# A mixture-of-experts stage on one core: the expert weights stand in TensorE instead of the rows, and each expert moves as many rows as its place in a ranking allows

## What is computed

```python
N_EXPERTS, TOP_K, EXPERT_FF, MOE_BLOCK = 64, 6, 256, 128
def _routed_experts(xt, eidx, gates, w_gate, w_up, w_down):
    ...
    def step(acc, blk):
        tok, g, e = blk
        xb = xpad[tok]
        hid = jax.nn.silu(xb @ w_gate[e]) * (xb @ w_up[e])
        yb = (hid @ w_down[e]) * g[:, None]
        return acc.at[tok].add(yb.astype(acc.dtype)), None
```

## Time and profile before

| what | us |
|---|---|
| median of three runs | 2301.89 |
| the profiled execution's own time | 2310.06 |
| its span in the profile | 2307.7 |
| PE busy in the span | 2164.2 (94%) |
| DVE, ACT, POOL busy | 1405.2, 1129.7, 645.4 |

### The profile page before, as it was taken

The page is one execution under the profiler, slowest core; times in us unless marked ns, Lnnn a source line. Parts: engine busy times, 40 slices in busy tenths (PEclk is TensorE's granted clock), DMA queues, the critical chain, the costliest instruction groups (busy, mean ns, idle before and its releaser), DMA issues. The chain is left out here.

```text
span 2307.7 us, 34429 instructions
## 1 busy us (share of the span) xinstructions
PE 2164.2 (94%) x10800; PEld 1766.7 (77%) x10800; DVE 1405.2 (61%) x2590; ACT 1129.7 (49%) x1866; POOL 645.4 (28%) x597
## 2 busy tenths in 40 slices
PE   6999999999899999959999999999999999999970
PEld 5777778777678888747888888888888888888850
DVE  5444444444677877746666666666666666666638
ACT  4344334433533333215556565555655565655537
POOL 1111111111113233332333333333333333333310
PEclk9999999999899999969999999999999999999995
DMA  6101101012623323247999989999999998999958
GB/s 218 40 31 34 41 32 37 34 41 84 244 67 107 101 81 109 93 161 224 284 286 279 277 275 285 281 280 281 280 287 284 284 278 276 275 286 280 282 110 323
DMA packets 194561, 435.84 MB, mean 189 GB/s; under 512 B 35488, under 2 KB 40080, under 8 KB 193200
## 3 DMA queue, kind: packets, MB, share of 16 engines
q1 hardware_dynamic: 150928, 289.49, 36.8%
q0 software_dynamic: 43312, 144.90, 23.6%
q10 hardware_dynamic: 288, 1.05, 0.1%
HBM read 328.16 MB, written 109.39 MB: 190 GB/s over the span
## 5 line engine op out<-in xcount | busy, mean ns | idle before, releaser
L1706 PE MATMUL ex_psU<-ex_guh,ex_xh 128*128 128x512 f32 x1024 | 413.8, 404 | 3.7 <-DVE ex_xl L1691 3.7
L1708 PE MATMUL ex_psU<-ex_guh,ex_xl 128*128 128x512 f32 x1024 | 402.6, 393 | 0.0
L1707 PE MATMUL ex_psU<-ex_gul,ex_xh 128*128 128x512 f32 x1024 | 400.5, 391 | 0.0
L1555 POOL DMA_INDIRECT acc_d<-ex_y,ex_use x128 | 206.3, 1612 | 410.1 <-ACT ex_y L1618 348.9
L1708 PEld LDWEIGHTS ex_psU<-ex_guh,ex_xl 128*128 128x128 f32 x1024 | 193.1, 189 | 43.3
L1706 PEld LDWEIGHTS ex_psU<-ex_guh,ex_xh 128*128 128x128 f32 x1024 | 193.3, 189 | 40.7 <-DVE ex_xl L1691 4.3
L1707 PEld LDWEIGHTS ex_psU<-ex_gul,ex_xh 128*128 128x128 f32 x1024 | 193.9, 189 | 37.5
L1577 POOL DMA_INDIRECT ex_xg<-h_d,entries x128 | 199.3, 1557 | 59.2 <-issue 38.1
L1706 PE MATMUL ex_psY<-ex_dnh,ex_hdh 128*128 128x512 f32 x512 | 210.2, 411 | 1.7 <-DVE ex_hdl L1662 1.7
L1618 ACT ACTIVATE ex_y<-ex_psY 128x1024 f32<-128x1024 f32 x128 | 131.3, 1025 | 143.3 <-PE ex_psY L1708 143.3
L1708 PE MATMUL ex_psY<-ex_dnh,ex_hdl 128*128 128x512 f32 x512 | 200.0, 391 | 0.0
(11 more groups left out here) (351 smaller groups left out, 4400.1 us busy)
## 6 DMA issues: line engine op xcount, KB each, us to landing
mi_g_raw<-w_experts SPq DMA_DIRECT2D x96, 1024.0 KB, 11.8
mi_g_place<-w_experts SPq DMA_DIRECT2D x96, 1024.0 KB, 11.8
mi_xr<-xT SPq DMA_DIRECT2D x17, 512.0 KB, 3.5
acc_d<-de_acc SPq DMA_DIRECT2D x17, 512.0 KB, 13.3
h_d<-de_h POOLq DMA_DIRECT2D x17, 512.0 KB
ln_t<-acc_d SPq DMA_DIRECT2D x17, 512.0 KB, 5.8
y<-ln_t SPq DMA_DIRECT2D x17, 512.0 KB, 4.4
de_cr<-cat SPq DMA_DIRECT2D x16, 512.0 KB
```

The lines of the kernel that those rows point to most:

```text
L1555: nc.gpsimd.indirect_dma_start(out=io["acc_d"], out_offset=bass.IndirectOffsetOnAxis(ap=use[:, k, 0:1].bitcast(U32), axis=0), in_=y[:, k, ...
L1706: nc.tensor.matmul(out, lh, rh, start=start, stop=False)
L1707: nc.tensor.matmul(out, lh, rl, start=False, stop=False)
L1708: return nc.tensor.matmul(out, ll, rh, start=False, stop=stop)
```

## The change

**Ranking.** The dense stage's end sorts the experts by their number of rows (two small products and some ten small DVE operations more, before the list of further blocks). Experts 0 and 1 keep the places 0 and 1, since their weights are loaded before the ranks are known; the other 62 follow by rising count. Each place has a capacity; an expert with more rows than its place takes gets further blocks of 256.

```diff
-OVMAX = 50
+OVMAX = 64
 OVP = OVMAX // 2
+MORE = NE + 2 * OVMAX
+CLASSES = ((1, 6, 176), (6, 13, 192), (13, 18, 208), (18, 23, 220), (23, 27, 236), (27, 32, 256))
+CAPS = [BLK] * 2 + [n for begin, end, n in CLASSES for _ in range(2 * (end - begin))]
...
-            sp.wait_ge(S["blocks_dve"], 3)
+            sp.wait_ge(S["blocks_dve"], 5)
```

(begin, end) are pairs of places, the third number is the capacity n of both places of such a pair. `pairs` writes pair 0 out and then, for each class, its first pair, and loops over the others of the class:

```diff
+            pair(0, BLK, BLK, None)
+            before = BLK
+            for begin, end, n in CLASSES:
+                peeled = 1
+                pair(begin, before, n, None)
+                if end > begin + peeled:
+                    with eng.Fori(begin + peeled, end) as p:
+                        pair(p, n, n, None)
+                before = n
```

SP reads the number of the expert from the table of the order (a value load for each expert), and takes weights that lie in DRAM as 8 KB in one piece for each partition instead of four pieces of 2 KB:

```diff
-                        w = io["w_experts"][bass.ds(e, 1), kind].rearrange("o k p n -> (o p) k n")
-                        sp.dma_start(raw[b][:, kind].rearrange("p (k n) -> p k n", k=4), w).then_inc(s_w[b][kind], 16)
+                        w = io["w_experts"][bass.ds(e, 1), kind].rearrange("o p n -> (o p) n")
+                        sp.dma_start(raw[b][:, kind], w).then_inc(s_w[b][kind], 16)
```

POOL keeps its order; the second gather and the second addition of an expert have n - 128 rows instead of 128 (`rows_of`):

```diff
+        rows_of = lambda n, t: P if t == 0 else n - P
...
                         nc.gpsimd.indirect_dma_start(
-                            out=xg[:, k, :], out_offset=None, in_=io["h_d"],
-                            in_offset=bass.IndirectOffsetOnAxis(ap=ent[:, k, 0:1].bitcast(U32), axis=0)).then_inc(s_row[k], 16)
+                            out=xg[0:r, k, :], out_offset=None, in_=io["h_d"],
+                            in_offset=bass.IndirectOffsetOnAxis(ap=ent[0:r, k, 0:1].bitcast(U32), axis=0)).then_inc(s_row[k], 16)
```

PE: in gate and up the weights stand and the rows move, n at once; the hidden values come out already transposed, so hidden_T and psH are gone. The unit of PE's order is now an expert, in two halves f of the hidden width:

```diff
+            def gate_up(e, b, f, n):
+                if not exists(e):
+                    return
+                if f == 0:
+                    pe.wait_ge(s_xl, 2 * e + 2)
+                after(pe, s_hid, 2 * e + f - 1)
+                for half in range(2):
+                    c0 = half * FF + f * P
+                    for kc in range(KC):
+                        if f == 0 and half == 0 and kc % 2 == 0:
+                            pe.wait_ge(s_split, 6 * e + kc // 2 + 1)
+                        last = three(psU[:, f, half, 0:n], guh[:, b, kc, c0:c0 + P], gul[:, b, kc, c0:c0 + P],
+                                     xh[:, kc, 0:n], xl[:, kc, 0:n], kc == 0, kc == KC - 1)
                 last.then_inc(s_gu, 1)
...
+            def pair(p, n1, n, j):
+                for b in range(2):
+                    e = 2 * p + b
+                    gate_up(e - 1, 1 - b, 1, n if b else n1)
+                    transpose_x(p, e, b)
+                    down(e - 2, b, n1)
+                    gate_up(e, b, 0, n)
```

```diff
+            def pair(p, n1, n, j):
+                for b in range(2):
+                    e, m = 2 * p + b, n if b else n1
+                    sigmoid(e - 1, 0, m)
+                    round_w(p, e, b, (0, 1))
+                    hidden(e - 1, 0, 1 - b, m)
+                    round_w(p, e, b, (2, 3))
+                    sigmoid(e - 1, 1, m)
+                    round_x(e, 0, n)
+                    hidden(e - 1, 1, 1 - b, m)
+                    round_x(e, 1, n)
+                    output(e - 2, b, range(4), n1)
+                    round_w(p, e, b, (4, 5))
```

More of the change, by code:

```diff
@@ L1648, in _, with sigmoid @@
-            end = pairs(act, pair)
-            n = 4 * end
-            hidden(n - 2)
-            sigmoid(n - 1, 3)
-            output(n - 2, 2, False)
-            hidden(n - 1)
-            output(n - 1, 3, False)
+            A = nc.scalar.activation
+            def sigmoid(e, f, n):
+                if exists(e):
+                    act.wait_ge(s_gu, 2 * e + f + 1)
+                    after(act, s_hid, 2 * e + f - 1)
+                    A(sg[:, f, 0:n], psU[:, f, 0, 0:n], ACT.Sigmoid).then_inc(s_sig, 1)
@@ L1656, in _ @@
+            e = 2 * pairs(act, pair)
+            sigmoid(e - 1, 0, BLK)
+            hidden(e - 1, 0, 1, BLK)
+            sigmoid(e - 1, 1, BLK)
+            output(e - 2, 0, range(2), BLK)
+            hidden(e - 1, 1, 1, BLK)
+            output(e - 2, 0, range(2, 4), BLK)
+            output(e - 1, 1, range(4), BLK)
         @block.vector
@@ L1701, in _ @@
+            e = 2 * pairs(dve, pair)
+            for f in range(FC):
+                activate(e - 1, f, BLK)
+                hidden(e - 1, f, 1, BLK)
         @block.tensor
@@ L1734, in down @@
+            def down(e, b, n):
+                if not exists(e):
+                    return
+                pe.wait_ge(s_hl, 2 * e + 2)
+                pe.wait_ge(s_split, 6 * e + 6)
+                for u in range(4):
+                    t, half = u // 2, u % 2
+                    r = rows_of(n, t)
+                    after(pe, s_y, 4 * e + u - 1)
                     for f in range(FC):
-                        last = three(psY[:, cols], hdh[:, f, :], hdl[:, f, :], dnh[:, b, f, cols], dnl[:, b, f, cols],
+                        last = three(psY[0:r, half, :], hdh[:, b, f, t * P:t * P + r], hdl[:, b, f, t * P:t * P + r],
+                                     dnh[:, b, f, half * 512:(half + 1) * 512], dnl[:, b, f, half * 512:(half + 1) * 512],
@@ L1760, in _, with pair @@
-            end = pairs(pe, pair)
-            n = 4 * end
-            hidden_T(n - 2, 2)
-            gate_up(n - 1, 3, 1, 12 * end - 2)
-            down(n - 2, 1, 12 * end)
-            hidden_T(n - 1, 3)
-            down(n - 1, 1, 12 * end)
+                    last.then_inc(s_dn, 1)
+            def pair(p, n1, n, j):
+                for b in range(2):
+                    e = 2 * p + b
[3 more added lines that the diff above has]
+                    gate_up(e, b, 0, n)
@@ L1770, in stage_norm @@
+            e = 2 * pairs(pe, pair)
+            gate_up(e - 1, 1, 1, BLK)
+            down(e - 2, 0, BLK)
+            down(e - 1, 1, BLK)
 def stage_norm(nc, io):
```

324 lines of the change are left out of this document (144 added, 180 removed).

## The result

The kernel became **slower**: 2362.05 us at the median (four runs, 2354.63 to 2365.87) beside 2304.33 for the kernel before on the same chips, a ratio of 1.024 with a 95% interval of 1.0221 to 1.0259. Forecast were 2272, in a range of 2225 to 2345. The profiled execution has a span of 2352.9 us.

The account below looks back on a forecast made before the run. PE was taken to bound the expert stage, with the DMA engines close behind. Experts save 36 + 1 us, the stage's ends cost 4 and 3: 30 less than the median of 2301.89 gives 2272 us, range 2225 to 2345.

Parts of the forecast that it names:

- p: Distance on PE between two gate and up products: 0.112 us under 256 columns, 0.119 at 256.
- Rivals 2, 3 and 5: Product distances on PE: 0.097 us, about 2243 (chance 0.13); 0.119 throughout, 2306 (0.09); 0.174, about 2580 (0.06).
- 7.2 + 96 p: PE's time for one expert: down products and transposes 7.2 us, plus 96 gate and up products; 17.95 for narrower experts.
- Gathers landing in under 6 us behind the additions: POOL's row gathers in the expert loop, with weights issued behind them, were expected to land in under 6 us.
- rival 1: Gathers, issued on POOL after additions, come too late if landing takes over 6.0 us; about 2530 at 10.4; chance 0.20.
- rival 4: Second gathers and additions of 92 rows use 4 of 16 DMA engines: 35 to 60 us, about 2315; chance 0.10.
- The sum: Expert stage's total: 37 us gained over the experts, less 4 and 3 at its ends, 30 us less in all.
- The ends: Start and end of the expert stage: 4 us more at the start, 3 us more at the end.
- The ranking and the layout at no cost: Ranking operations hidden before the table's entries load; 8 KB weight pieces costed at nothing, since nothing waits for weights.

Follow-up runs that it names:

- experiment 4: Changed kernel, second gather and addition both rounded up to 96 and 112 rows, capacities 220 and 236 kept: 2281.7 us, ratio 0.9912 to the kernel before.
- experiment 8: Kernel before with only the weights' layout changed, 8 KB in one piece instead of four of 2 KB: 2302.81 us, ratio 0.9992.
- experiment 1: Changed kernel with capacities 220 and 236 raised to 224 and 240: 2287.11 us, ratio 0.9914 to the kernel before.
- experiment 7: Changed kernel with only two classes, 52 experts with 240 rows and the others with 256: 2300.22 us, ratio 0.9992 to the kernel before.

## Why the prediction was wrong, point by point

- **p, right.** Forecast 0.112 under 256 columns and 0.119 at 256; measured 0.111 to 0.112 for 176 to 240, and 0.120. The reading that the load of the stationary operand sets it fits: the width makes no difference below 256 columns. The estimate of 0.107 by the Trainium skill (TensorE: Matmul & The Clock Gate, LDWEIGHTS (loading the stationary operand)) is close below. Rivals 2, 3 and 5 are out.
- **7.2 + 96 p, right, with an error of 0.1.** Forecast 17.95, measured 18.05 in the first three classes. Over the 52 narrow experts experiment 4, where nothing else disturbs, takes 941.9 us against 970.0 before: 28 saved, forecast 36. Some 5 of the 8 missing us lie in those 0.1, the others in the classes of 220 and 236, at 18.2 and 18.4.
- **Gathers landing in under 6 us behind the additions, right for the good row counts only in its effect.** In experiment 4 a gather takes 4.2 to 7.7, 6.1 at the median, so about half take longer than forecast; PE waits 2.2 us in all. The weights are indeed issued behind them. The deciding point of rival 1, a landing of 6 us, is where its waits begin; so it has no slack, and that is why rival 4 hit so hard.
- **The failed step: the row counts.** The sum has no term for them, which puts a transfer of 92 or 108 rows at the price of 128 in proportion; they stand in rival 4 alone, with a chance of 0.10. The mechanism was written down rightly there, 92 rows on 4 engines. The Trainium skill's rule (DMA: Bandwidth & Descriptors, Why a DMA increments its semaphore by 16 and not by 1) holds for these indirect transfers by GpSimd: 4 engines for 92 and 76 rows are slow, 10 for 100 a little, 12 to 15 for 108, 52, 60 and 84 hardly or not. Its exception for some direct copies from GpSimd doesn't reach them. The rival's price was too low, 3.5 to 6 us for each of 10 experts. The two slow transfers follow each other and hold up the gather of 128 rows between them (landings 6 to 10.9), two experts behind the class still pay, and a wait of 4.1 us costs 1.7 us more by the clock. Measured: 66.7 us over twelve experts, beside experiment 4. The forecast of 2272 with that is 2339, with the 8 us above and the 3 below 2350; of the 12 left, 2.7 are in the class of 236 (113.2 us for its last six experts, 110.5 in experiment 4), 2 are that before ran at 2304 on these chips, not 2302, and 7 are that the 66.7 come from an execution of 2354.63 us, 7.4 below the median.
- **The ends, 7 forecast, about 10 measured** in experiment 4: the stage from the load of the entries to the next stage takes 1211.35 us instead of 1228.59, so 17.2 less; 28 less by the narrow experts, about 0.8 more by the nine of 256 columns between the last of them and expert 63, leaves 10. A part that I did not see is a wait at the very end, in the kernel after:

```profile
2257.28 0.38 PE L1745 MATMUL ex_psU<-ex_xh,ex_guh 128*128 128x256 f32 x1 [4.03 <-issue]
```

  PE leaves the loop there with nothing in flight that the profile names, 4.03 us (4.27 in experiment 4). What it is, no run tested. Before, the same place shows 1.43.
- **The ranking and the layout at no cost, right.** The layout by experiment 8. The first entries are loaded at 1015.36 us after the change, at 1019.18 before it and at 1013.24 in experiment 8, which has no ranking.

The net for good row counts, on the same chips, is 21 us in experiment 4 (2281.7 instead of 2303.07) and 18 in experiment 1 (2287.11 instead of 2305.43), against 30 forecast. With 224 and 240 in the place of 220 and 236 the time would have come out 15 us above the forecast, well inside its range.

## What to carry to other kernels

Check how many DMA engines a row count can be shared by before it is made a parameter: four rows more (92 to 96, 220 to 224) were worth 75 us. A slow transfer is not local: those issued behind it on the queue wait too, and TensorE pays for each stall again in clock, here 1.7 us on 4.1. And before a size is refined for one engine, look for which engine it pays: the narrow classes gave TensorE nothing below 256 columns, but gave the DMA engines the room that made the gain.

## What was not expected of the hardware

- Rounding one of the two slow transfers recovers 15 or 35 of 80 us, both together all of it.
- q0's packets: 44048 with the odd counts and 38096 with both rounded, for 122.87 and 123.43 MB, though the engine time is the same (8960 and 8937 us). In the trace the surplus is packets of 4 and 8 bytes, 3048 of each. More packets at no cost in engine time; why they are made, no run tells.
- The DMA engines are nearer to being the bound than PE's 9 tenths let see: at a share of 0.94 and 280 GB/s (experiment 7) PE waited for gathers 27 times, only one point above the 0.93 of the earlier trace rows, where the old order had slack for a landing of 10.4 us.
